# A modulation vector summed on VectorE instead of TensorE, in a two-layer fp32 transformer kernel

## The chip, the cores and the metric

The program runs on one core of one Trainium2 chip. The metric is the device time of one execution in microseconds (us). The kernel before takes 1998.46 us, the median of three runs (1994.62 to 2003.45). The profile below is of one further execution, which took 1997.8 us; its span, from the first to the last recorded instruction, is 1996.1 us.

## The reference, cut to what matters

Two layers act on x of 256 tokens by 2048 features. The first layer begins with an adaptive norm: a vector c of 2048 numbers, through silu and a large matrix, gives a shift, a scale and a gate of 2048 numbers each. All is fp32.

```python
mod = jax.nn.silu(c) @ w_ada + b_ada                 # w_ada: 2048 x 6144
shift, scale, gate = jnp.split(mod, 3, axis=-1)
h = _rms_norm(x, g_norm) * (1.0 + scale[:, None, :]) + shift[:, None, :]
proj = h @ w_in                                      # w_in: 2048 x 9296
```

What follows (two attentions, an output product, a second layer with a recurrent mixer, latent attention and a feed-forward block) is not touched by the change. Only shift and scale matter here, that is 4096 columns of w_ada (33.6 MB); the gate's columns are read and summed later, in the old way.

## The kernel before, in words

**Engines.** Each engine has its own instruction list, and semaphores order them. SyncE (SP) issues all large loads, in the order in which they are written. TensorE (PE) multiplies. ScalarE (ACT) copies each loaded piece of a weight to a rounded high part (`high`, L1474). GpSimd (POOL) subtracts that from the piece to get the low part (`low_part`, L545). VectorE (DVE) splits activations in the same way (L1883, L1884).

**Pieces.** A product in fp32 accuracy is made of three products of high and low parts (L865, L866, L867). A weight piece is 512 rows of 512 columns (1 MB; four slots in `WR`, two in `WH`). ScalarE and GpSimd handle it in two halves of 128x1024.

**The head of the kernel.** The 2048 features are taken in four quarters of 512. For quarter q the kernel needs shift and scale of those 512 features, that is 1024 columns of w_ada over all 2048 rows. It reads them in eight pieces, numbers 8q to 8q+7, each 256 rows by 1024 columns in two loads of 512 KB, into four slots `ada_w` (`ada_quarter`, L605). `mod_piece` (L934) multiplies each piece on TensorE: four matmuls of 512 columns, each with 32 stationary columns that all hold silu(c), so that four groups of PSUM partitions hold four partial rows. After the eighth piece ScalarE copies the bank to `mod_row` (L1533), `mod_cols` (L942) turns the row into columns, VectorE adds the bias (L1875) and forms the gain (L1878), ScalarE scales the four transposed blocks of x (L1537), and VectorE splits them into `HX` (L1883, L1884). Then four weight pieces of `w_in` for those 512 rows can be multiplied (`piece`): (q,0) has 128 columns, (q,1) and (q,2) have 512 and give transposed output, (q,3) has 512 and gives token-major output. Below, "piece (q,i)" is one of these, and "the end of the head" is the last product of piece (3,3). After it follow the remaining columns of `w_in`, with the same three helpers.

**What sets the order.** It is written out by hand. On TensorE the products of the next quarter's modulation stand between the four pieces (3, 2, 2 and 1 of them). On SyncE the loads of the next quarter's eight modulation pieces stand between the loads of this quarter's pieces. A modulation slot is free again when `ada_done` has counted its piece, a `WR` slot when `piece_done` has. GpSimd and ScalarE take the pieces of `w_in` in order; the high part of piece n waits for TensorE to have done piece n-2.

**The start.** Before the first quarter, SyncE also issues 24 small parameter loads (L625 to L633), x is normalised, and TensorE transposes x through a diagonal matrix (L976), which ScalarE copies to `xT` (L1500).

Of the kernel before, what the change touches and what calls it, by code (L numbers as in the profile page):

```python
# [21 lines left out]
ALU = mybir.AluOpType  # L22
ACT = mybir.ActivationFunctionType
# [3 lines left out]
P = 128  # L27
# [3 lines left out]
KT = D // P  # L31
# [15 lines left out]
CH = 512  # L47
# [87 lines left out]
def build(nc, a, out):  # L135
    ctx = ExitStack()
    with ctx:
# [38 lines left out]
        def at(off, *shape):  # L176
            n = int(np.prod(shape))
            assert off + n <= ARENA, (off, n)
            v = arena[:, off:off + n]
            used[0] = off + n  # L180
            if len(shape) == 1:
                return v
            names = "abcd"[:len(shape)]
            return v.rearrange(f"p ({' '.join(names)}) -> p {' '.join(names)}",
                               **{m: s for m, s in zip(names[1:], shape[1:])})
# [45 lines left out]
        mod_row = at(4096, CH)  # L231
        CA = at(4608, KT, 32)
# [6 lines left out]
        half_col = small[:, 400:402]  # L239
        ones = level0T  # L240
# [335 lines left out]
        def _(sp):  # L576
# [57 lines left out]
            ada_quarter(0, 4, 8)  # L634
            for q in range(4):
                in_piece(q, 0)
                in_piece(q, 1)
                if q < 3:
                    ada_quarter(q + 1, 0, 3)
                in_piece(q, 2)  # L640
                if q < 3:
                    ada_quarter(q + 1, 3, 5)
                in_piece(q, 3)
                if q < 3:
                    ada_quarter(q + 1, 5, 8)
# [197 lines left out]
        def _(pe):  # L843
# [82 lines left out]
            def mod_piece(n):  # L926

                i = n % 8
                pe.wait_ge(ada_in[n % 4], 32 * (n // 4 + 1))
                if i == 0 and n >= 8:  # L930
                    pe.wait_ge(mod_ready, n // 8)
                for g in range(4):
                    o = slice(32 * g, 32 * g + 32)
                    last = pe.matmul(BANK[0][o, :], CA[:, 2 * i + g // 2, :], ada_w[n % 4][:, g * CH:(g + 1) * CH],  # L934
                                     start=i == 0, stop=i == 7)
                last.then_inc(ada_done, 1)

            def mod_cols(m):

                pe.wait_ge(row_took, m + 1)  # L940
                for j in range(4):
                    last = pe.matmul(BANK[0][:, 2 * j:2 * j + 2], mod_row[:, j * P:(j + 1) * P], half_col,  # L942
                                     start=True, stop=True)
                last.then_inc(mod_cols_ready, 1)
# [54 lines left out]
            pe.wait_ge(c_wide, 1)  # L999
            for n in range(4):  # L1000
                mod_piece(n)

# [7 lines left out]
            for n in range(4, 8):  # L1010
                mod_piece(n)
            for q in range(4):
                more = 8 * (q + 1)
                mod_cols(q)
                for i, (token, first, width) in enumerate(((False, 1, P), (False, 4, CH), (False, 6, CH), (True, 2, CH))):
                    if q < 3:
                        for n in range(*((0, 3), (3, 5), (5, 7), (7, 8))[i]):
                            mod_piece(more + n)
                    piece(n_in + 4 * q + i, q, token, first, width)
                    if q == 3 and i == 1:  # L1020
                        pe.wait_ge(kiT_taken, 1)
                        for t in range(TT):
                            last = pe.transpose(BANK[0][:, t * P:t * P + P], KIT[:, t * P:(t + 1) * P], ident[:])
                        last.then_inc(ki_ready, 1)
# [47 lines left out]
            pe.wait_ge(c_wide, 2)  # L1072
# [24 lines left out]
            pe.wait_ge(row_took, 5)  # L1097
# [357 lines left out]
        def _(act):  # L1455
# [75 lines left out]
            for q in range(4):  # L1531
                act.wait_ge(ada_done, 8 * (q + 1))
                act.activation(mod_row, BANK[0][:, :], ACT.Copy).then_inc(row_took, 1)  # L1533
                high(n_in + 4 * q)
                act.wait_ge(mod_ready, q + 1)
                for k in range(4 * q, 4 * q + 4):
                    act.activation(xT[:, k, :], xT[:, k, :], ACT.Identity, bias=mod[:, k:k + 1],  # L1537
                                   scale=gs[:, k:k + 1]).then_inc(x_scaled, 1)
                high(n_in + 4 * q + 1)
                if q == 3:  # L1540
                    act.wait_ge(piece_done, n_in + 13)
                    act.activation(KIT, BANK[1][:, 0:L], ACT.Copy).then_inc(kiT_taken, 1)
                high(n_in + 4 * q + 2)
                high(n_in + 4 * q + 3)
# [278 lines left out]
        def _(dve):  # L1823
# [34 lines left out]
            spread_c(CA)  # L1858
            own.link(dve.tensor_tensor(half_col, group_col[:, 0:2], group_col[:, 2:4], ALU.add))
            norm_dve(0)  # L1860
            make_diag(0)
            dve.wait_ge(colsT_ready, 1)
# [9 lines left out]
            for q in range(4):  # L1872
                o = slice(4 * q, 4 * q + 4)
                dve.wait_ge(mod_cols_ready, q + 1)
                own.link(dve.tensor_tensor(two_rows(mod[:, 0:2 * KT])[:, :, o],  # L1875
                                           BANK[0][:, 0:8].rearrange("p (j h) -> p h j", h=2),
# [471 lines left out]
```

## Time and profile before

| what | value |
|---|---|
| median of three runs | 1998.46 us |
| the profiled execution's own time | 1997.8 us |
| its span | 1996.1 us |
| TensorE busy | 1900.8 us (95% of the span) |
| GpSimd busy | 1322.8 us (66%) |
| VectorE busy | 893.0 us (45%) |
| ScalarE busy | 810.7 us (41%) |
| end of the head | 168.7 us after the start |

Busy time is the sum of an engine's recorded instructions. A recorded duration begins when the instruction is taken up by its engine, so it can contain a time in which the engine is held up. The granted clock (PEclk) is the mean clock that TensorE was given in a stretch, 1.00 being 2.4 GHz. In the timeline view, "x8" merges eight neighbouring instructions of one line; an fp32 matmul leaves two records. "idle before" names what the engine waited for.

### The profile page before, as it was taken

What the parts mean: (1) busy time and instruction counts of PE and PEld (TensorE: products, weight loads), DVE (VectorE), ACT (ScalarE), POOL (GpSimd) and SP (SyncE); (2) the same over time, 40 slices, a digit from 0 to 9 for tenths busy, and PEclk for the clock granted to TensorE, in tenths of its full rate; (3) what the DMA queues carried; (4) which work ended last, traced back from release to release, by engine and by line L of the source; (5) the groups of instructions that cost most, each with busy time, mean ns of one, the idle gap of its engine ahead of it and who ended that gap; (6) DMA issues with size and microseconds to landing.
All of it is one profiled execution on the core that took longest, in us unless ns stands there. A gap on an engine that the chain in (4) does not pass through costs nothing.

```text
span 1996.1 us, 32360 instructions
## 1 busy us (share of the span) xinstructions
PE 1900.8 (95%) x13023; PEld 1590.4 (80%) x13023; DVE 893.0 (45%) x1122; ACT 810.7 (41%) x1095; POOL 1322.8 (66%) x677
## 2 busy tenths in 40 slices
PE   5889999999989899999999999999999999999997
PEld 2668878888658798877699877888888888888886
DVE  1005547560442424556644251654455555733323
ACT  3234444444444454333422343443443433434333
POOL 2448878888139499863544386798888888844442
PEclk9899999999999999999999999999999999999999
DMA  9985545555765356543100145555555555555553
GB/s 340 360 294 169 190 159 178 190 190 190 288 209 178 116 169 208 183 136 128 43 25 4 46 168 168 169 186 181 182 187 189 189 182 182 184 195 198 195 190 126
DMA packets 174434, 352.60 MB, mean 177 GB/s; under 512 B 6736, under 2 KB 19422, under 8 KB 171774
## 3 DMA queue, kind: packets, MB, share of 16 engines
q1 hardware_dynamic: 173437, 346.94, 52.4%
q10 hardware_dynamic: 896, 4.20, 0.5%
q8 instruction: 78, 1.28, 0.3%
q14 instruction: 23, 0.18, 0.0%
HBM read 349.02 MB, written 2.10 MB: 176 GB/s over the span
## 4 chain that ended last, share of the span: by engine, by line
PE 59%; POOL 20%; issue 18%; DVE 2%; ACT 1%; POOLq 0%; DVEq 0%; ACTq 0%
PE bank L911 21%; POOL WL L545 19%; PE bank L913 10%; PE bank L865 6%; PE bank L866 6%; PE bank L867 6%; PE bank L1257 5%; PE bank L1177 1%; PE bank L1187 1%; PE bank L1220 1%; PE bank L393 0%; POOLq L544 0%; DVE arena L2192 0%; POOL arena L812 0%; PE bank L1364 0%
## 5 line engine op out<-in xcount | busy, mean ns | idle before, releaser
L545 POOL TENSOR_TENSOR WL<-WR,WH 128x1024 fp32r<-128x1024 f32 (+2 forms) x516 | 1227.8, 2390 | 495.2 <-ACT WH L1474 493.9
L1474 ACT ACTIVATE WH<-WR 128x1024 fp32r<-128x1024 f32 (+2 forms) x560 | 577.3, 1037 | 815.6 <-PE bank L867 451.8
L911 PE MATMUL bank<-HX,WH 128*128 128x512 f32 x1840 | 651.8, 399 | 6.9 <-POOL WL L545 5.3
L913 PE MATMUL bank<-HX,WL 128*128 128x256 f32 x1840 | 516.6, 281 | 0.0
L911 PEld LDWEIGHTS bank<-HX,WH 128*128 128x128 f32 x1840 | 345.8, 188 | 93.8 <-issue 6.0
L865 PE MATMUL bank<-WH,HX 128*128 128x512 f32 (+2 forms) x864 | 340.2, 394 | 11.3 <-POOL WL L545 6.3
L913 PEld LDWEIGHTS bank<-HX,WL 128*128 128x128 f32 x1840 | 347.6, 189 | 0.0
L866 PE MATMUL bank<-WL,HX 128*128 128x512 f32 (+2 forms) x864 | 332.5, 385 | 0.0
L867 PE MATMUL bank<-WH,HX 128*128 128x512 f32 (+2 forms) x864 | 332.5, 385 | 0.0
L865 PEld LDWEIGHTS bank<-WH,HX 128*128 128x128 f32 x864 | 163.7, 189 | 48.1 <-issue 13.3
L866 PEld LDWEIGHTS bank<-WL,HX 128*128 128x128 f32 x864 | 163.9, 190 | 31.3 <-issue 1.9
L867 PEld LDWEIGHTS bank<-WH,HX 128*128 128x128 f32 x864 | 163.7, 190 | 31.2
L2037 DVE TENSOR_REDUCE arena<-bank 128x256 f32<-128x512 f32 x115 | 71.5, 684 | 251.9 <-PE bank L913 251.9
L865 PE MATMUL bank<-WH,AH 128*128 128x512 f32 x352 | 136.9, 389 | 0.0
L866 PE MATMUL bank<-WL,AH 128*128 128x512 f32 x352 | 136.9, 389 | 0.0
L867 PE MATMUL bank<-WH,AL 128*128 128x512 f32 x352 | 136.9, 389 | 0.0
L545 DVE TENSOR_TENSOR WL<-WR,WH 128x1024 fp32r<-128x1024 f32 x44 | 53.9, 1226 | 159.0 <-ACT WH L1474 159.0
L1960 DVE TENSOR_SCALAR arena<-arena,small 128x128 f32<-128x128 f32 x64 | 63.7, 1065 | 47.8 <-ACT small L1482 47.8
L2275 DVE SCALAR_TENSOR_TENSOR arena<-arena,cols 128x256 f32<-128x256 f32 x44 | 83.3, 1950 | 1.5
L865 PEld LDWEIGHTS bank<-WH,AH 128*128 128x128 f32 x352 | 66.1, 188 | 13.8
L867 PEld LDWEIGHTS bank<-WH,AL 128*128 128x128 f32 x352 | 66.1, 188 | 13.7
L866 PEld LDWEIGHTS bank<-WL,AH 128*128 128x128 f32 x352 | 66.1, 188 | 13.5
(292 smaller groups left out, 1954.1 us busy)
## 6 DMA issues: line engine op xcount, KB each, us to landing
WR<-in_w_in SPq DMA_DIRECT2D x96, 1024.0 KB, 5.0
WR<-in_ffn_w_gate SPq DMA_DIRECT2D x44, 1024.0 KB, 5.1
WR<-in_ffn_w_up SPq DMA_DIRECT2D x44, 1024.0 KB, 5.2
WR<-in_ffn_w_down SPq DMA_DIRECT2D x44, 1024.0 KB, 5.1
arena<-in_w_ada SPq DMA_DIRECT2D x64, 512.0 KB, 9.8
WR<-in_w_out SPq DMA_DIRECT2D x32, 1024.0 KB, 5.1
WR<-in_w_ada SPq DMA_DIRECT2D x16, 1024.0 KB, 5.1
WR<-in_w_in SPq DMA_DIRECT2D x12, 768.0 KB, 4.3
```

Source lines behind the costliest of these rows:

```text
L545: eng.tensor_tensor(half(WL, n % NSLOT, *w), half(WR, n % NSLOT, *w), half(WH, nth(n) % 2, *w), ALU.subtract).then_inc(ready, 1)
L865: pe.matmul(out, stat[0], mov[0], start=start, stop=False, skip_group_check=True)
L866: pe.matmul(out, stat[0], mov[1], start=False, stop=False, skip_group_check=True)
L867: return pe.matmul(out, stat[1], mov[0], start=False, stop=stop, skip_group_check=True)
L911: pe.matmul(bank[:, :].rearrange("p (h n) -> p h n", h=2), wh[:, k, o], HX[:, :, kk, :], start=kk == 0, stop=False, skip_group_check=True)
L913: last = pe.matmul(bank[:, 0:L], wl[:, k, o], HX[:, 0, kk, :], start=False, stop=kk == KT - 1, skip_group_check=True)
L1177: last = pe.matmul(BANK[h // 2][:, (h % 2) * L:(h % 2 + 1) * L], w[h // 2][:, k, (h % 2) * stride:(h % 2) * stride + P], CT[:, c0 + k, :], ...
L1257: last = pe.matmul(o[h, q, :], x(h, q), y(h, q), start=(n == 0), stop=(n == len(terms) - 1))
L1474: act.activation(half(WH, nth(n) % 2, *w), half(WR, n % NSLOT, *w), ACT.Copy).then_inc(hi_ready, 1)
L1960: last = dve.tensor_scalar(v, v, hr[:, g:g + 1], None, ALU.mult)
L2037: dve.tensor_reduce(dst, BANK[bank][:, :].rearrange("p (h n) -> p n h", h=2), AX_X, ALU.add).then_inc(ready, 1)
L2275: last = dve.scalar_tensor_tensor(out=CV[:, f, :], in0=RAWF[:, f, 0:L], scalar=w(0), in1=CV[:, f, :], op0=ALU.mult, op1=ALU.add)
```

## The change

Three things change, all in the head.

1. The modulation sums leave TensorE. `mod_add` on VectorE takes each of the 32 pieces in two instructions of 128x1024: the loaded half times silu(c) as a scalar per partition, added to `mod_sum` (the first of a quarter is a plain multiply). After eight pieces `mod_sum` holds 128 partial sums for each of 1024 columns. `mod_cols` multiplies it with a column of ones: eight matmuls of 2 columns in the place of four. `mod_piece`, the copy of the bank to `mod_row` and the widening of silu(c) (`spread_c(CA)`) go.
2. SyncE's order is new: pieces (q,0) and (q,1) are loaded ahead of the last modulation pieces of quarter q, and (q,2), (q,3) among the first ones of quarter q+1.
3. ScalarE makes the high parts of (q,0) and (q,1) before it waits for the gains of quarter q.

```diff
-            ada_quarter(0, 4, 8)
-            for q in range(4):
+            in_piece(0, 0)
+            ada_quarter(0, 4, 7)
+            in_piece(0, 1)
+            ada_quarter(0, 7, 8)
+            for q in range(1, 4):
+                ada_quarter(q, 0, 2)
+                in_piece(q - 1, 2)
+                ada_quarter(q, 2, 4)
+                in_piece(q - 1, 3)
+                ada_quarter(q, 4, 6)
                 in_piece(q, 0)
+                ada_quarter(q, 6, 7)
                 in_piece(q, 1)
-                if q < 3:
-                    ada_quarter(q + 1, 0, 3)
...
+                ada_quarter(q, 7, 8)
+            in_piece(3, 2)
+            in_piece(3, 3)
...
             def mod_cols(m):
 
-                pe.wait_ge(row_took, m + 1)
+                pe.wait_ge(ada_done, 8 * (m + 1))
                 for j in range(4):
-                    last = pe.matmul(BANK[0][:, 2 * j:2 * j + 2], mod_row[:, j * P:(j + 1) * P], half_col,
-                                     start=True, stop=True)
+                    for h in range(2):
+                        o = slice(h * CH + j * P, h * CH + (j + 1) * P)
+                        last = pe.matmul(BANK[0][:, 4 * j + 2 * h:4 * j + 2 * h + 2], mod_sum[:, m % 2, o], ones[:, 0:2],
+                                         start=True, stop=True)
...
             for q in range(4):
-                act.wait_ge(ada_done, 8 * (q + 1))
-                act.activation(mod_row, BANK[0][:, :], ACT.Copy).then_inc(row_took, 1)
                 high(n_in + 4 * q)
+                high(n_in + 4 * q + 1)
                 act.wait_ge(mod_ready, q + 1)
...
+            def mod_add(n):
+
+                q, i = n // 8, n % 8
+                total = mod_sum[:, q % 2, :]
+                dve.wait_ge(ada_in[n % 4], 32 * (n // 4 + 1))
+                for k in range(2):
+                    w = ada_w[n % 4][:, k * 2 * CH:(k + 1) * 2 * CH]
+                    cc = cs[:, 2 * i + k:2 * i + k + 1]
+                    ins = (dve.tensor_scalar(total, w, cc, None, ALU.mult) if i + k == 0 else
+                           dve.scalar_tensor_tensor(out=total, in0=w, scalar=cc, in1=total, op0=ALU.mult, op1=ALU.add))
+                    if k == 0:
+                        own.link(ins)
+                ins.then_inc(ada_done, 1)
+                dve.wait_ge(ada_done, n + 1)
+
+            mod_add(0)
+            mod_add(1)
             norm_dve(0)
             make_diag(0)
+            for n in range(2, 6):
+                mod_add(n)
...
             for q in range(4):
                 o = slice(4 * q, 4 * q + 4)
+                for n in range(8 * q if q else 6, 8 * q + 8):
+                    mod_add(n)
                 dve.wait_ge(mod_cols_ready, q + 1)
```

VectorE's list between the first quarter's split and the second quarter's gain, before. `HX` is the split activation, `small` holds the gains, `cols` the parameters.

```order
L1883 CAST HX<-arena 128x512
L1884 TENSOR_TENSOR HX<-arena,HX 128x512
L1875 TENSOR_TENSOR small<-bank,cols 128x2x4
L1878 SCALAR_TENSOR_TENSOR small<-small,cols 128x4
L1883 CAST HX<-arena 128x512
```

The same place in the changed kernel, where `arena` in the new rows is both `mod_sum` and the loaded slot `ada_w`.

```order
L1883 CAST HX<-arena 128x512
L1884 TENSOR_TENSOR HX<-arena,HX 128x512
L1847 TENSOR_SCALAR arena<-arena,small 128x1024
L1848 SCALAR_TENSOR_TENSOR arena<-arena,small 128x1024 x15
L1875 TENSOR_TENSOR small<-bank,cols 128x2x4
L1878 SCALAR_TENSOR_TENSOR small<-small,cols 128x4
L1883 CAST HX<-arena 128x512
```

Sixteen instructions of 128x1024 now stand between the split of one quarter and the gain of the next.

SyncE's list behind the small parameter loads, before. The loads of 128x2x512 are halves of w_ada's pieces, those of 128x4x128 are pieces (q,0), those of 128x4x512 the other pieces of w_in.

```order
L605 DMA arena<-in_w_ada 128x2x512 x8
L581 DMA WR<-in_w_in 128x4x128
L581 DMA WR<-in_w_in 128x4x512
L605 DMA arena<-in_w_ada 128x2x512 x6
L581 DMA WR<-in_w_in 128x4x512
L605 DMA arena<-in_w_ada 128x2x512 x4
L581 DMA WR<-in_w_in 128x4x512
```

And in the changed kernel.

```order
L579 DMA WR<-in_w_in 128x4x128
L603 DMA arena<-in_w_ada 128x2x512 x6
L579 DMA WR<-in_w_in 128x4x512
L603 DMA arena<-in_w_ada 128x2x512 x6
L579 DMA WR<-in_w_in 128x4x512
L603 DMA arena<-in_w_ada 128x2x512 x4
L579 DMA WR<-in_w_in 128x4x512
L603 DMA arena<-in_w_ada 128x2x512 x4
L579 DMA WR<-in_w_in 128x4x128
```

Piece (0,0) is now loaded ahead of w_ada's pieces 4 to 6, and piece (0,1) ahead of piece 7; pieces (1,0) and (1,1) come ahead of w_ada's last two and last piece of their quarter.

## Rows read from the trace of the kernel before

**Rows 1.** The page's first part: busy time, share of the span, instructions.

```profile
PE 1900.8 (95%) x13023; PEld 1590.4 (80%) x13023; DVE 893.0 (45%) x1122; ACT 810.7 (41%) x1095; POOL 1322.8 (66%) x677
```

**Rows 2.** Windows from each quarter's gain to the next, then the head's end.

```profile
core 0: us, PE busy (x) PEld busy (x) DVE busy (x) ACT busy (x) POOL busy (x), PEclk, DMA share, GB/s
40.00:80.30 40.30, 34.52 (x204) 23.00 (x204) 2.16 (x5) 9.24 (x13) 15.61 (x8) 0.79 1.02 369
80.30:112.60 32.30, 29.19 (x204) 20.98 (x204) 2.47 (x6) 9.23 (x13) 15.63 (x8) 0.95 1.02 367
112.60:143.30 30.70, 27.87 (x204) 20.17 (x204) 2.48 (x6) 9.23 (x13) 15.69 (x8) 1.00 0.80 282
143.30:168.70 25.40, 21.97 (x134) 20.14 (x134) 12.08 (x16) 13.88 (x21) 20.50 (x9) 0.87 0.50 166
```

**Rows 3.** Timeline of VectorE from 36 to 180 us: start, duration, what.

```profile
39.42 0.47 DVE L1878 SCALAR_TENSOR_TENSOR small<-small,cols 128x4 f32<-128x4 f32 x1
...
80.29 0.17 DVE L1875 TENSOR_TENSOR small<-bank,cols 128x8 f32<-128x8 f32 x1 [37.02 <-PE bank L942]
80.49 0.16 DVE L1878 SCALAR_TENSOR_TENSOR small<-small,cols 128x4 f32<-128x4 f32 x1
...
83.34 0.69 DVE L1884 TENSOR_TENSOR HX<-arena,HX 128x512 fp32r<-128x512 f32 x1
...
143.54 0.16 DVE L1878 SCALAR_TENSOR_TENSOR small<-small,cols 128x4 f32<-128x4 f32 x1
```

**Rows 4.** Timeline of TensorE around the last quarter's start and end.

```profile
142.35 0.95 PE L942 MATMUL bank<-small,arena 128*128 128x2 f32 x8
146.06 0.39 PE L865 MATMUL bank<-HX,WH 128*128 128x256 f32 x1 [2.77 <-DVE HX L1884]
...
149.44 0.55 PE L865 MATMUL bank<-HX,WH 128*128 128x256 f32 x1 [0.66 <-POOL WL L545]
...
168.32 0.39 PE L867 MATMUL bank<-WH,HX 128*128 128x512 f32 x1
```

**Rows 5.** Groups by line and shape from 36 to 150 us.

```profile
L545 POOL TENSOR_TENSOR WL<-WR,WH 128x1024 fp32r<-128x1024 f32 x20 | 47.5, 2390 | 40.5 <-ACT WH L1474 40.4
...
L934 PE MATMUL bank<-arena 128*32 128x512 f32 x208 | 30.6, 688 | 12.5 <-DMA arena<-in_w_ada 11.4 <-DVE small L1878 1.1
...
L545 POOL TENSOR_TENSOR WL<-WR,WH 128x256 fp32r<-128x256 f32 x8 | 5.7, 731 | 52.3 <-ACT WH L1474 52.3
```

**Rows 6.** VectorE groups by line and shape, whole run.

```profile
L545 DVE TENSOR_TENSOR WL<-WR,WH 128x1024 fp32r<-128x1024 f32 x44 | 53.9, 1226 | 159.0 <-ACT WH L1474 159.0
...
L2246 DVE CAST AH<-arena 128x1024 fp32r x8 | 5.5, 687 | 0.0
...
L2139 DVE SCALAR_TENSOR_TENSOR Bv<-Bv,RA 128x2048 f32<-128x2048 f32 x1 | 2.3, 2291 | 0.0
```

**Rows 7.** Timelines of VectorE and GpSimd, 1700 to 1715 us, in the feed-forward block.

```profile
1704.45 2.62 DVE L2246 CAST AH<-arena 128x1024 fp32r<-128x1024 f32 x1 [0.21 <-DVE arena L2287]
1707.10 3.32 DVE L2247 TENSOR_TENSOR AL<-arena,AH 128x1024 fp32r<-128x1024 f32 x1
1710.34 2.88 DVE L2246 CAST AH<-arena 128x1024 fp32r<-128x1024 f32 x1
1713.26 3.31 DVE L2247 TENSOR_TENSOR AL<-arena,AH 128x1024 fp32r<-128x1024 f32 x1
...
1703.59 11.88 POOL L545 TENSOR_TENSOR WL<-WR,WH 128x1024 fp32r<-128x1024 f32 x4 [0.43 <-ACT WH L1474]
```

**Rows 8.** A scalar_tensor_tensor of 256 columns with GpSimd busy beside it.

```profile
L2086 DVE SCALAR_TENSOR_TENSOR arena<-arena,cols x24: 472/2370/2718, 781.2 to 895.4; 128x256 f32 x24
```

**Rows 9.** Windows of 10 us.

```profile
20.00:30.00 10.00, 7.97 (x46) 5.85 (x47) 1.09 (x8) 1.79 (x3) 0.00 (x0) 1.00 0.92 310
30.00:40.00 10.00, 8.47 (x73) 5.47 (x71) 0.64 (x2) 4.27 (x9) 1.41 (x2) 1.00 1.05 368
...
70.00:80.00 10.00, 10.00 (x63) 8.05 (x62) 0.00 (x0) 1.21 (x3) 1.43 (x2) 1.00 1.05 389
```

**Rows 10.** Timeline of ScalarE: the last copy of x's transposes.

```profile
33.94 0.60 ACT L1500 ACTIVATE arena<-bank 128x512 f32<-128x512 f32 x1 [0.41 <-PE bank L976]
```

**Rows 11.** TensorE's timeline, piece (0,1), which follows waits: first and later products.

```profile
57.08 0.58 PE L865 MATMUL bank<-HX,WH 128*128 128x256 f32 x1
...
60.87 0.41 PE L867 MATMUL bank<-HX,WL 128*128 128x256 f32 x1
...
61.49 0.28 PE L867 MATMUL bank<-HX,WL 128*128 128x256 f32 x1
```

More of the change, by code:

```diff
@@ L230, in build @@
         kin_g = at(24992, IDX_DIM)
-        mod_row = at(4096, CH)
-        CA = at(4608, KT, 32)
+        mod_sum = at(4096, 2, 2 * CH)
         ada_w = [at(8192 + PK * CH * i, PK * CH) for i in range(4)]
@@ L238, in build @@
         group_col = ident[:].rearrange("p (g m) -> p g m", m=32)[:, :, 0]
-        half_col = small[:, 400:402]
         ones = level0T
@@ L633, in _ @@
             sp.dma_start(kin_g, a["k_norm_idx"][0:1, :].to_broadcast([P, IDX_DIM])).then_inc(params_in, 16)
-            ada_quarter(0, 4, 8)
-            for q in range(4):
+            in_piece(0, 0)
[8 more added lines that the diff above has]
+                ada_quarter(q, 4, 6)
                 in_piece(q, 0)
+                ada_quarter(q, 6, 7)
                 in_piece(q, 1)
-                if q < 3:
-                    ada_quarter(q + 1, 0, 3)
[L640 to L645, printed above, removed]
+                ada_quarter(q, 7, 8)
+            in_piece(3, 2)
+            in_piece(3, 3)
             with sp.Fori(1, 8) as j:
@@ L924, in ada_piece @@
                 last.then_inc(piece_done, 1)
[L926 to L936, printed above, removed]
             def mod_cols(m):
-                pe.wait_ge(row_took, m + 1)
+                pe.wait_ge(ada_done, 8 * (m + 1))
                 for j in range(4):
-                    last = pe.matmul(BANK[0][:, 2 * j:2 * j + 2], mod_row[:, j * P:(j + 1) * P], half_col,
-                                     start=True, stop=True)
+                    for h in range(2):
+                        o = slice(h * CH + j * P, h * CH + (j + 1) * P)
+                        last = pe.matmul(BANK[0][:, 4 * j + 2 * h:4 * j + 2 * h + 2], mod_sum[:, m % 2, o], ones[:, 0:2],
+                                         start=True, stop=True)
                 last.then_inc(mod_cols_ready, 1)
@@ L997, in _ @@
             pe.transpose(BANK[7][:, 0:KT], c_rows[0:KT, :], ident[0:KT, 0:KT]).then_inc(cT_ready, 1)
-            pe.wait_ge(c_wide, 1)
-            for n in range(4):
-                mod_piece(n)
             pe.wait_ge(params_in, PARAM_DMAS * 16)
@@ L1009, in _ @@
                 to_feature(X, g, 4, 0, scaled=True)
-            for n in range(4, 8):
-                mod_piece(n)
             for q in range(4):
-                more = 8 * (q + 1)
                 mod_cols(q)
                 for i, (token, first, width) in enumerate(((False, 1, P), (False, 4, CH), (False, 6, CH), (True, 2, CH))):
-                    if q < 3:
-                        for n in range(*((0, 3), (3, 5), (5, 7), (7, 8))[i]):
-                            mod_piece(more + n)
                     piece(n_in + 4 * q + i, q, token, first, width)
@@ L1070, in _ @@
                         last.then_inc(headT_ready, 1)
-            pe.wait_ge(c_wide, 2)
+            pe.wait_ge(c_wide, 1)
             pe.wait_ge(act_took, ACT_RKV)
@@ L1096, in _ @@
             turn_y(1)
-            pe.wait_ge(row_took, 5)
+            pe.wait_ge(row_took, 1)
             gate_chunk(0)
@@ L1538, in _ @@
                                    scale=gs[:, k:k + 1]).then_inc(x_scaled, 1)
-                high(n_in + 4 * q + 1)
                 if q == 3:
@@ L1857, in _ @@
             dve.wait_ge(cs_ready, 1)
-            spread_c(CA)
-            own.link(dve.tensor_tensor(half_col, group_col[:, 0:2], group_col[:, 2:4], ALU.add))
+            def mod_add(n):
[13 more added lines that the diff above has]
+            mod_add(1)
             norm_dve(0)
             make_diag(0)
+            for n in range(2, 6):
+                mod_add(n)
             dve.wait_ge(colsT_ready, 1)
@@ L1873, in _ @@
                 o = slice(4 * q, 4 * q + 4)
+                for n in range(8 * q if q else 6, 8 * q + 8):
+                    mod_add(n)
                 dve.wait_ge(mod_cols_ready, q + 1)
                 own.link(dve.tensor_tensor(two_rows(mod[:, 0:2 * KT])[:, :, o],
-                                           BANK[0][:, 0:8].rearrange("p (j h) -> p h j", h=2),
+                                           BANK[0][:, 0:16].rearrange("p (j h two) -> p h j two", h=2, two=2)[:, :, :, 0],
                                            two_rows(col("b_ada", 0, 2 * KT))[:, :, o], ALU.add))
```

## The prediction

> **What bounds the kernel now.** I read the page's busy shares first: TensorE is busy 95% of the span [rows 1], so outside the head it sets the time, and the change touches only the head. So the question is when the head ends. I then cut the head at each quarter's gain [rows 2]. Column by column the reader is to see: the transfers run at 369 and 367 GB/s with a share of 1.02 in the first two stretches and 282 in the third; TensorE is busy 34.5 of 40.3, 29.2 of 32.3 and 27.9 of 30.7 us; GpSimd is busy 15.6 us in each; VectorE only 2.2 to 2.5 us. Transfers and TensorE are both near their end, and VectorE is nearly empty. A stretch of 10 us with full transfers shows 389 GB/s [rows 9]; a quarter needs 8.39 MB of w_ada and 3.41 MB of w_in, 11.80 MB, which is 30.3 us at that rate. The gains are made at 39.9, 80.65 and 143.7 us [rows 3], and the last product of the head ends at 168.7 us [rows 4].
>
> **What the change removes.** TensorE loses the modulation's products: 208 records, 30.6 us, between 36 and 150 us [rows 5]. Of this little reaches the end by itself, because the transfers leave only 30.3 us as the least for a quarter against cadences of 32.3 and 30.7. ScalarE's copy of the bank and its wait go, too. All that could be won is set by the transfers, and is worked out under the third rival.
>
> **What it adds.** Per quarter VectorE gets one multiply and 15 multiply-adds of 128x1024. No row has a multiply-add of exactly this shape. The one of 2048 columns takes 2.291 us and an addition-type instruction of 1024 columns takes 1.226 [rows 6], so a multiply-add of 1024 lies between 1.15 (half of 2.291) and 1.226; I take 1.22, and 0.03 for each wait on its own semaphore (80.29 + 0.17 to 80.49 [rows 3]). The multiply takes 0.69, as the cast of the same shape [rows 6]. Sum: 0.69 + 15 x 1.25 = 19.4 us. Behind it stands a chain in which VectorE does nothing else: eight matmuls of 2 columns, twice the four that take 0.95 [rows 4], with the hand-over 2.0 us; the gain, from 80.29 to 80.65, 0.36; ScalarE's scaling and the split, until 84.03, 3.4 us [rows 3]. Together 25.2 us for a quarter if nothing holds VectorE up. That is less than the 30.3 of the transfers, so taken alone the change would be hidden behind them.
>
> **What holds it up.** GpSimd makes the low parts in the same 114 us: 20 of 2.39 us and 8 of 0.73 [rows 5], 15.6 us in each quarter [rows 2]. In the feed-forward block both engines work at once on the same shapes [rows 7]. A VectorE instruction with two inputs in SBUF that takes 1.226 by itself [rows 6] there takes 3.31 and 3.32, the cast 2.62 and 2.88 in place of 0.69; the four GpSimd instructions take 11.88 in place of 4 x 2.39 = 9.56. The excess of 2.3 is a cast and a tensor_tensor and a cast, 0.6 + 1.1 + 0.6. So the engines take turns, instruction by instruction, and each waits for the whole of the other's. The multiply-add does the same: with 256 columns it has a median of 2.37 us beside GpSimd against a least of 0.472 [rows 8]. The price of a GpSimd instruction that meets a multiply-add is therefore its full 2.39 us on VectorE's chain.
>
> The Trainium skill says this as a rule that speaks against the change (SBUF — State Buffer, "Who interferes with whom"): an instruction of VectorE with two SBUF inputs and a GpSimd instruction that reads SBUF exclude each other for their whole length. By that rule the sum is the one below; if only casts and multiplies excluded GpSimd, it would be the third rival's.
>
> The cadence of a quarter is then 25.2 plus what GpSimd does while VectorE has work. All 15.6 us may meet it: 40.8. Or GpSimd fills the 3.5 us in which VectorE waits for the eight matmuls and for ScalarE's first two scalings: 37.3. Pieces (q,0) and (q,1) now get their low parts before the gain, among the last multiply-adds, and the high part of (q,2) waits for TensorE to have done half of (q,0), so its low parts begin when the next quarter's adds do. Little falls into the gap; I take 39.5. VectorE no longer waits for loads, as 39.5 is more than 30.3; the transfers wait for it.
>
> **The first quarter.** At 20.4 us pieces 0 to 3 have arrived as before (there VectorE keeps up: 2.5 us a piece against 2.7 for its transfer). Now (0,0), pieces 4 to 6, (0,1) and piece 7 must come, 5.5 MB; 3.1 MB arrive by 30 us and the rest at 0.37 MB/us by 36.5 [rows 9]. ScalarE is free at 34.5 [rows 10] and makes high parts at once; GpSimd follows from 35.3 with 0.73, 0.73, 2.39, 2.39. The two adds of piece 7 meet them: 36.5 + 2.5 without a collision, two of 2.39 more with both. With the eight matmuls and the gain this is 41.3 to 46.2; I take 44.5, against 39.9 before: +4.6 us.
>
> **The last quarter's products.** Before, 2.4 us passed from the gain to the first product, then 22.6 to the end [rows 4]. The narrow piece ran from 146.06 to 148.8, there was a wait of 0.66 for GpSimd, and (3,1) ran to 157.3 at a lower clock (0.87 over the stretch [rows 2]). Piece (0,1) shows the size: after waits its products come at 0.21 us, and at 0.12 from 61.4 on [rows 11], 4.3 us at 1.2 GHz and then 2.4. In the changed kernel TensorE waits longer before the gain, so this is met once, but (3,1) is ready: 2.7 + 6.9 + 6.0 + 5.6 = 21.2, a gain of 1.4.
>
> **The sum.** The last gain comes at 44.5 + 3 x 39.5 = 163.0 against 143.7. The head ends at 163.0 + 2.4 + 21.2 = 186.6 against 168.7, +17.9 us, and nothing behind it changes. On the profiled execution's 1997.8 us this is 2015.7, predicted as 2016. The median of the runs shown is 0.7 us above that execution, which changes nothing. The own range: with 41.3, 37.3 and 21.2 the head ends at 176.8, with 46.2, 40.8 and 22.6 at 193.6; so 2006 to 2023.
>
> **The rivals.** What a measurement of this kernel can tell from no change is about 0.5%, 10 us.
>
> First, the engines share instead of taking turns: each slows the other, and a meeting costs half. The cadence is 25.2 + 7.8 = 33.0, the head ends at 44.5 + 99 + 23.6 = 167.1, -1.6 us: 1996. For it speaks only that no row has this instruction at 1024 columns beside GpSimd; rows 7 speak against it. 6%.
>
> Second, TensorE's clock. It now works about 21 of 39.5 us per quarter and waits for the rest. Should it stay at 1.2 GHz, its 19.3 us of products (1.7 + 6.0 + 6.0 + 5.6) become 38.6, and with the 2.0 for the columns and the 3.5 until the first product the cadence is 44, bound by TensorE: 44.5 + 132 + 2.4 + 38.6 = 217.5, +49, 2046. Against it: after a wait the clock came back within 4.3 us of work [rows 11]. 5%.
>
> Third, on the other side: the multiply-add does not exclude GpSimd's subtraction, or GpSimd's work falls almost wholly into VectorE's waits. Then the transfers bound each quarter at 30.3, the first gain comes at 41.3, the last at 132.2, and the head ends at 155.8: -12.9, 1985. It is the case if a quarter's meetings cost under 5 us; the change breaks even where they cost 8.3 of the 15.6 (44.5 + 3 x 33.5 + 23.6 = 168.6). Half of GpSimd's work would have to miss VectorE, which is idle 3.5 us in a quarter. 7%. The Trainium skill advises about 358 GB/s for transfers from HBM (SBUF — State Buffer, "Summary: rules for kernel authors"); by it a quarter is 33.0 us and this rival's estimate 1993. The trace has 389, so the rival keeps 1985.
>
> **How the numbers follow.** The forecast has 82%; of it about 76 points lie above 2008.5 and 6 below. Faster by over 0.5% (below 1988.5) is the third rival: 7%. Within 0.5%: the first rival and the forecast's lower edge, 12%. Slower: 76 and the second rival's 5, 81%. The range 2002 to 2024 holds the forecast with a little on either side for how runs scatter, about 8 in 10; the rivals lie outside.
>
> **What would show it.** The multiply-adds of 128x1024 come in two sizes, about 1.22 and 3.3 to 3.6 us, with a mean near 2.2; GpSimd's 2.39 becomes longer, too. The gains lie about 39.5 us apart, VectorE is busy or held nearly all of a quarter's time, and the transfers fall to about 300 GB/s. TensorE has a gap of over 10 us per quarter that ends with VectorE's `ada_done`. Wrong would be: every multiply-add at 1.22 with VectorE waiting for w_ada (third rival), a mean near 1.7 (first), or products at 0.21 us all through a quarter (second). Were the last gain at 163 and the end of the head not 23.6 us later, my tail would be wrong.

## The result, and the profile after

The changed kernel takes 2025.6 us in the median of four runs (2021.2 to 2032.7), against 2001.0 us for the kernel before in four (1994.6 to 2005.4). The ratio is 1.0143, 95% interval 1.0116 to 1.0170: 1.4% slower, 23 to 34 us; the two medians lie 24.7 us apart. Forecast were 2016 us and a range of 2002 to 2024: the direction was right, the size was too small, and the median lies 1.6 us above the range.

The profiled execution took 2032.7 us, its span is 2031.0. First the windows from one gain to the next, then the head's end; the columns are those of [rows 2], which they answer.

```profile
core 0: us, PE busy (x) PEld busy (x) DVE busy (x) ACT busy (x) POOL busy (x), PEclk, DMA share, GB/s
47.80:89.80 42.00, 24.82 (x148) 23.43 (x148) 33.74 (x22) 9.06 (x12) 20.45 (x8) 0.74 0.82 284
89.80:130.50 40.70, 24.36 (x148) 22.97 (x148) 35.16 (x22) 9.06 (x12) 21.38 (x8) 0.75 0.82 287
130.50:171.10 40.60, 24.49 (x148) 23.10 (x148) 33.78 (x22) 9.06 (x12) 20.95 (x8) 0.75 0.67 235
171.10:194.80 23.70, 21.28 (x136) 20.27 (x137) 10.60 (x15) 12.00 (x20) 15.82 (x7) 0.84 0.40 134
```

A quarter lasts 42.0, 40.7 and 40.6 us, where it lasted 40.3, 32.3 and 30.7. VectorE, which was busy 2.2 to 2.5 us, is now busy or held 33.7 to 35.2; the same eight GpSimd instructions, 15.6 us before, take 20.5 to 21.4; the transfers have fallen from 369 to 284 GB/s. The granted clock is 0.74 to 0.75 of full. Next the multiply-adds of the whole run (count, least, median and longest duration in ns, what the engine waited for before them) and GpSimd's low parts from 50 to 150 us.

```profile
L1848 DVE SCALAR_TENSOR_TENSOR arena<-arena,small x60: 1276/1285/3317, 12.7 to 163.8; 128x1024 f32<-128x1024 f32 x60
...
  DMA arena<-in_w_ada: 9.5, 5
```

```profile
L543 POOL TENSOR_TENSOR WL<-WR,WH 128x1024 fp32r<-128x1024 f32 x16 | 48.7, 3072 | 48.8 <-ACT WH L1456 48.8
...
L543 POOL TENSOR_TENSOR WL<-WR,WH 128x256 fp32r<-128x256 f32 x4 | 5.5, 1402 | 2.5 <-ACT WH L1456 2.5
```

A multiply-add takes 1.28 us when it is alone and up to 3.32 beside GpSimd; GpSimd's 2.39 [rows 5] has become 3.07 in the mean. Both are held by the other. One instruction of each, from the middle of a run of such meetings, in the third quarter:

```profile
97.37 3.38 POOL L543 TENSOR_TENSOR WL<-WR,WH 128x1024 fp32r<-128x1024 f32 x1
98.52 3.31 DVE L1848 SCALAR_TENSOR_TENSOR arena<-arena,small 128x1024 f32<-128x1024 f32 x1
```

The next two begin at 100.72 and 101.87, so a pair lasts 3.35 us, where one after the other would need 1.28 + 2.39 = 3.67. The engines take turns, but a meeting costs VectorE 2.03 us (3.31 - 1.28) and not the full 2.39. The timeline of VectorE, with the gains that answer to [rows 3]:

```profile
37.61 6.06 DVE L1848 SCALAR_TENSOR_TENSOR arena<-arena,small 128x1024 f32<-128x1024 f32 x2 [1.87 <-DMA arena<-in_w_ada]
47.41 0.17 DVE L1875 TENSOR_TENSOR small<-bank,cols 128x8 f32<-128x8 f32 x1 [3.73 <-PE bank L934]
47.60 0.16 DVE L1878 SCALAR_TENSOR_TENSOR small<-small,cols 128x4 f32<-128x4 f32 x1
...
80.59 5.08 DVE L1848 SCALAR_TENSOR_TENSOR arena<-arena,small 128x1024 f32<-128x1024 f32 x2 [2.46 <-DMA arena<-in_w_ada]
...
93.85 32.52 DVE L1848 SCALAR_TENSOR_TENSOR arena<-arena,small 128x1024 f32<-128x1024 f32 x15
...
170.99 0.16 DVE L1878 SCALAR_TENSOR_TENSOR small<-small,cols 128x4 f32<-128x4 f32 x1
```

Fifteen multiply-adds, 19.8 us of work with their waits (15 x 1.32), last 32.5. In the quarter of 42.0 us VectorE also waits 2.5 us for w_ada, and in the last one 1.4, which the forecast had excluded. And before each gain VectorE waits 3.73 us for TensorE's column matmuls. TensorE's timeline shows them, and the start and the end of the last quarter's products, as [rows 4] did:

```profile
85.73 3.58 PE L934 MATMUL bank<-level0T,arena 128*128 128x2 f32 x16 [14.35 <-DVE arena L1848]
...
167.11 3.57 PE L934 MATMUL bank<-level0T,arena 128*128 128x2 f32 x16 [13.36 <-DVE arena L1848]
...
194.36 0.40 PE L869 MATMUL bank<-WH,HX 128*128 128x512 f32 x1
```

The eight matmuls take 3.57 us, in the first quarter after 9.3 us of idle time and in the others after 13 to 14. The granted clock over them, and over the four matmuls of the kernel before (the column behind the instruction counts is PEclk):

```profile
85.73:89.31 3.58, 3.57 (x16) 3.49 (x16) 0.00 (x0) 0.00 (x0) 0.00 (x0) 0.50 1.05 386
142.35:143.30 0.95, 0.95 (x9) 0.86 (x7) 0.00 (x0) 0.00 (x0) 0.00 (x0) 1.00 0.00 0
```

It is 0.50, that is 1.2 GHz, in the changed kernel and 1.00 in the kernel before. The head ends at 194.8 us, 26.1 us later than the 168.7 of before. What is left of the profiled executions' difference of 34.9 us, 8.8, lies behind the head, where both kernels run the same instructions; it is taken up below.

### The profile page after: what moved, and what is told of

The parts are those of the page before. It is cut to its first block, busy times and chain, and to the rows that moved or that the text cites. A ratio compares the mean times of both kernels' runs of the same rounds, so it can differ in the third digit from the quotient of the medians.

```text
span 2031.0 us, 31997 instructions
## 1 busy us (share of the span) xinstructions
PE 1883.4 (93%) x12799; PEld 1604.2 (79%) x12799; DVE 1018.7 (50%) x1184; ACT 810.7 (40%) x1091; POOL 1340.1 (66%) x677
## 4 chain that ended last, share of the span: by engine, by line
PE 59%; POOL 20%; issue 18%; DVE 2%; ACT 1%; POOLq 0%; DVEq 0%; ACTq 0%
PE bank L913 20%; POOL WL L543 20%; PE bank L915 10%; PE bank L867 6%; PE bank L868 6%; PE bank L869 6%; PE bank L1239 5%; PE bank L1159 2%; PE bank L1169 1%; PE bank L1202 1%; PE bank L969 0%; PE bank L391 0%; DVE arena L2192 0%; POOLq L542 0%; DVE arena L2322 0%
## 5 line engine op out<-in xcount | busy, mean ns | idle before, releaser
L543 POOL TENSOR_TENSOR WL<-WR,WH 128x1024 fp32r<-128x1024 f32 (+2 forms) x516 | 1245.2, 2424 | 503.1 <-ACT WH L1456 502.0
L1848 DVE SCALAR_TENSOR_TENSOR arena<-arena,small 128x1024 f32<-128x1024 f32 x60 | 116.0, 1934 | 11.8 <-DMA arena<-in_w_ada 9.5
```

Source lines behind the costliest of these rows:

```text
L543: eng.tensor_tensor(half(WL, n % NSLOT, *w), half(WR, n % NSLOT, *w), half(WH, nth(n) % 2, *w), ALU.subtract).then_inc(ready, 1)
L1848: dve.scalar_tensor_tensor(out=total, in0=w, scalar=cc, in1=total, op0=ALU.mult, op1=ALU.add))
```

## The experiments

The theory after the result: the two engines take turns instruction by instruction, as forecast, and the part that the forecast missed is that the column matmuls run at the lower clock. "Head's end" is the last product of piece (3,3) in the run's profile; a ratio is to the kernel before, timed beside it.

**low_small.** GpSimd's work in the head is made short.

```diff
-            eng.tensor_tensor(half(WL, n % NSLOT, *w), half(WR, n % NSLOT, *w), half(WH, nth(n) % 2, *w),
+            eng.tensor_tensor(cut(half(WL, n % NSLOT, *w)), cut(half(WR, n % NSLOT, *w)), cut(half(WH, nth(n) % 2, *w)),
                               ALU.subtract).then_inc(ready, 1)     # cut: v[:, :, 0:32] in the head
-                wh, wl = view(WH, nth(n) % 2, width), view(WL, n % NSLOT, width)
+                wh = wl = view(WH, nth(n) % 2, width)
```

> The changed kernel, but in the head GpSimd subtracts only 32 columns of each weight piece instead of 512 or 128, and TensorE multiplies the high part in the low part's place (the head's low products are left out). Turn-taking theory: the multiply-adds all come at 1.25 us or less, the gains are 25.2 + 1.7 (the column matmuls took 3.6 us, not 2.0) + about 1.5 of short GpSimd instructions = 28.4 us apart if nothing else binds, so the loads bind at 30.3 to 31; head's end near 43.5 + 3 x 31 + 23.6 = 160 us against 194.8 in the changed kernel, the ratio to the kernel before about 0.995. Rival (VectorE's sums are slow by themselves, or the low clock of TensorE is what costs): gains stay 38 us or more apart, ratio above 1.01.

Measured: ratio 0.9935 (0.9918 to 0.9952), head's end 161.4. The multiply-adds of this run, and the timeline around its second gain:

```profile
L1851 DVE SCALAR_TENSOR_TENSOR arena<-arena,small x60: 1276/1285/1348, 12.7 to 132.2; 128x1024 f32<-128x1024 f32 x60
```

```profile
44.41 0.16 DVE L1881 SCALAR_TENSOR_TENSOR small<-small,cols 128x4 f32<-128x4 f32 x1
...
68.85 2.61 DVE L1851 SCALAR_TENSOR_TENSOR arena<-arena,small 128x1024 f32<-128x1024 f32 x2 [2.33 <-DMA arena<-in_w_ada]
75.19 0.17 DVE L1878 TENSOR_TENSOR small<-bank,cols 128x8 f32<-128x8 f32 x1 [3.73 <-PE bank L937]
75.39 0.16 DVE L1881 SCALAR_TENSOR_TENSOR small<-small,cols 128x4 f32<-128x4 f32 x1
```

No multiply-add is above 1.35 us, VectorE waits for w_ada (2.33 us), and the gains are 31.0 us apart. The meetings with GpSimd are worth 33.4 us of head (194.8 - 161.4), more than the whole loss. VectorE's sums alone are fast enough.

**psum.** The same sums with only one tensor input in SBUF.

```diff
-                total = mod_sum[:, q % 2, :]
+                total = BANK[0][:, :]
...
+                for k in range(4):
+                    w = ada_w[n % 4][:, k * CH:(k + 1) * CH]
+                    kk = 4 * (i % 4) + k
+                    dst = mod_sum[:, q % 2, (i // 4) * CH:(i // 4 + 1) * CH] if kk == KT - 1 else total
...
+                           dve.scalar_tensor_tensor(out=dst, in0=w, scalar=cc, in1=total, op0=ALU.mult, op1=ALU.add))
```

> The changed kernel with the running sum in PSUM: w_ada is read as eight pieces of 512 rows by 512 columns, VectorE takes each in four multiply-adds of 512 columns whose second tensor input is PSUM bank 0, and only the last of 16 writes to mod_sum. So only one tensor input lies in SBUF. Turn-taking theory: these adds do not meet GpSimd; each takes 0.69 to 0.72 us, 32 of them 23 us, with 3.7 + 0.4 + 3.4 behind them 30.5 us a quarter, so the loads bind at 31; first gain near 45, head's end 45 + 3 x 31 + 23.6 = 161.6 us, ratio to the kernel before 0.995 to 0.997. Rival (any VectorE instruction with an SBUF tensor input and this much work is held by GpSimd, or the sheer work on VectorE costs): mean of an add above 1.1 us, gains 40 us or more apart, ratio above 1.01.

Measured: ratio 0.9997 (0.9973 to 1.0022), head's end 166.5, 28.3 us before the changed kernel's. Its multiply-adds, and VectorE's and GpSimd's groups from 50 to 150 us:

```profile
L1850 DVE SCALAR_TENSOR_TENSOR bank<-arena,small,bank x112: 747/756/757, 12.2 to 137.0; 128x512 f32<-128x512 f32 x112
```

```profile
L1850 DVE SCALAR_TENSOR_TENSOR bank<-arena,small,bank 128x512 f32<-128x512 f32 x83 | 62.7, 756 | 3.1 <-DMA arena<-in_w_ada 0.2
...
L543 POOL TENSOR_TENSOR WL<-WR,WH 128x1024 fp32r<-128x1024 f32 x19 | 45.0, 2383 | 55.2 <-ACT WH L1456 55.2
```

None of 112 adds is longer than 0.757 us, and GpSimd is back at 2.38: a multiply-add with one SBUF tensor input doesn't meet it. Those 112 also write to PSUM. The last add of each sum writes to SBUF and isn't held either, so it is the input that counts (from 35 to 150 us); nor is it the width, since adds of 256 columns are held in [rows 8]:

```profile
L1850 DVE SCALAR_TENSOR_TENSOR arena<-arena,small,bank 128x512 f32<-128x512 f32 x7 | 5.2, 748 | 0.2
```

The quarters are 32.6 us apart, not 31, since an add takes 0.756 and not 0.69, so that VectorE's chain binds: 32 x 0.79 + 3.7 + 0.4 + 3.4 = 32.8. That miss is 4.9 us of head (166.5 against 161.6), 0.25%; a head 2.2 us shorter than before is a ratio of 0.999, which the interval holds. This answers to the rule of the Trainium skill that the prediction drew on (SBUF — State Buffer, "Who interferes with whom"), by which a VectorE instruction with two SBUF inputs contends with a GpSimd instruction that reads SBUF. The trace agrees: up to 3.32 us with two such inputs, 0.757 at most with one.

**warm.** Idle-time matmuls ahead of the column matmuls.

```diff
+                for k, n in ((5, 12), (6, 12), (7, 9)):
+                    pe.wait_ge(ada_done, 8 * m + k)
+                    warm(n)                       # n matmuls of ident by ident into unread columns
                 pe.wait_ge(ada_done, 8 * (m + 1))
```

> The changed kernel with 33 idle-time matmuls of 128x128 in front of each mod_cols (after the adds of pieces 5, 6 and 7 of the quarter), written to columns of bank 0 that nobody reads. Clock theory: the eight column matmuls of a quarter take 1.9 us in place of 3.57, so each gain comes 1.7 us sooner, the first products of the quarter run at 0.12 us; head's end 4 x 1.7 + 1.5 = 8 us sooner, near 187 us, ratio to the kernel before about 1.009. Rival (matmuls of 2 columns into one bank cost that much at any clock): 3.6 us stays, head's end near 194, ratio 1.013. Turn-taking itself is not touched: multiply-adds beside GpSimd stay at 3.5 us.

Measured: ratio 1.0101 (1.0082 to 1.0120), head's end 191.0, half of what was expected. The first quarter's column matmuls took 1.95 us, the others 3.50, 3.26 and 2.72. TensorE's timeline (products left out) around its second gain:

```profile
78.41 2.27 PE L931 MATMUL bank<-ident 128*128 128x128 f32 x18 [1.62 <-DVE arena L1856]
83.02 3.50 PE L942 MATMUL bank<-level0T,arena 128*128 128x2 f32 x16 [2.34 <-DVE arena L1856]
```

TensorE was idle for 2.34 us between the fillers and the columns. The granted clock over the column matmuls of the four quarters:

```profile
43.78:45.73 1.95, 1.95 (x16) 1.87 (x16) 0.00 (x0) 0.00 (x0) 0.00 (x0) 0.96 1.05 385
83.02:86.52 3.50, 3.50 (x16) 3.41 (x16) 0.00 (x0) 0.00 (x0) 0.00 (x0) 0.52 1.05 386
123.71:126.96 3.25, 3.25 (x16) 3.17 (x16) 0.00 (x0) 0.00 (x0) 0.00 (x0) 0.56 1.05 387
164.09:166.81 2.72, 2.72 (x16) 2.64 (x16) 0.00 (x0) 0.00 (x0) 0.00 (x0) 0.68 0.00 0
```

The time follows the clock, so the clock theory stands. It does not follow the idle time just before: that was 2.02 us in the first quarter, 2.34 in the next two and 4.22 in the last. Fillers that leave a gap do not make the clock sure.

**warm2.** More fillers: `((5, 14), (6, 14), (7, 15))`, and `warm(9)` behind the columns.

> The changed kernel with more idle-time matmuls: 14, 14 and 15 behind the adds of pieces 4, 5 and 6 of a quarter and 9 behind the column matmuls. In the first run with such matmuls a gap of 1.6 to 4.2 us was left ahead of the column matmuls, which took 1.95, 3.50, 3.26 and 2.72 us. Clock theory: with the gap closed they take 1.9 to 2.1 in each quarter and the first products 0.12; gains about 39 us apart, head's end near 186, ratio 1.008. Rival (the matmuls' length does not hang on the clock before them): over 3 us again.

Measured: ratio 1.0101 (1.0063 to 1.0139), head's end 185.8. The column matmuls' records (two for each matmul), and one quarter's:

```profile
L942 PE MATMUL bank<-level0T,arena x64: 251/251/272, 44.0 to 163.0; 128*128 128x2 f32 x64
```

```profile
83.05 1.95 PE L942 MATMUL bank<-level0T,arena 128*128 128x2 f32 x16 [0.37 <-DVE arena L1857]
```

All are at 0.251 us against 0.353 in the changed kernel, 1.95 us for the eight, with a granted clock of 1.00 over them in the second quarter; the gains are 39.1 us apart, and the head ends 9.0 us sooner. With the clock that the forecast took for granted, the head ends near where the forecast had it (186.6), which is in part luck: the first gain is 1.9 us later than forecast, the three quarters together 1.1 and the tail 1.6 us shorter. The ratio is that of warm, whose head ended 5.2 us later, so what the second set of fillers adds is shown by the traces and not by the times.

**sums_only.** VectorE's sums, old orders of SyncE and ScalarE (the first and the fourth hunk of the diff undone).

> VectorE's sums with the load order and ScalarE's order of the kernel before. Turn-taking theory: the same GpSimd work meets the same adds, so the gains stay about 41 us apart; head's end 195 to 197 us (piece (q,1)'s low parts come after the gain), ratio to the kernel before 1.012 to 1.015, within 0.2% of the changed kernel. Rival (the new order of loads, which puts GpSimd's work beside the adds, is what costs): gains 33 to 36 us apart, ratio below 1.006.

Measured: ratio 1.0103 (1.0082 to 1.0125), head's end 186.9. The gains, at 40.9, 81.7, 122.4 and 163.4, are 40.8 us or more apart, so the cadence is not the order's, as the theory said. But the first gain is 6.9 us sooner, which my 195 to 197 had left out, and the ratio lies below the 1.012 to 1.015 expected. The head ends 7.9 us sooner than the changed kernel's, and 3.9 of them are given back at once: behind it TensorE waits 3.7 us for the index keys where the changed kernel went straight on and then waited 1.2, and the next products start at 192.4 against 196.4 us.

This run also shows the multiply that opens a quarter's sum beside GpSimd (GpSimd's low parts begin at 44.05 us, the multiply at 44.21):

```profile
L1843 DVE TENSOR_SCALAR arena<-arena,small x4: 752/2864/2872, 11.9 to 125.7; 128x1024 f32<-128x1024 f32 x4
```

It has one tensor input in SBUF and writes to SBUF, and still takes 2.86 us in place of 0.75, as the casts of [rows 7] did. So two SBUF inputs are what makes the multiply-adds meet GpSimd, but other instructions meet it with one.

**first_old.** The changed kernel with only the first quarter's loads as before (pieces 4 to 7 of w_ada, then (0,0) and (0,1)).

> The changed kernel with one thing undone: in the first quarter w_ada's pieces 4 to 7 are loaded ahead of w_in's pieces (0,0) and (0,1), as before. Theory (putting these two ahead delays piece 7 by their 1.3 MB and brings their low parts beside its adds): first gain 41 to 42.5 us in place of 47.8, later gains still 40.7 to 42 apart, head's end 187.5 to 190 against 194.8, ratio to before 1.009 to 1.011. Rival (the low parts must meet some adds anyway, so the first quarter's saving is given back in the second): first gain early, but the second still near 89.8, head's end 194, ratio 1.013.

Measured: ratio 1.0094 (1.0060 to 1.0127), gains at 41.7, 83.4, 124.1 and 164.8, head's end 188.6. The 6.2 us of the first quarter are kept to the end. So of the changed kernel's loss 6 us come from two loads put ahead of w_ada's in the first quarter.

**order_only.** The kernel before with the new orders, TensorE's sums kept (the first and the fourth hunk alone).

> TensorE's sums of the kernel before with the new load order and ScalarE's new order. Turn-taking theory: without VectorE's adds nothing is lost; piece (q,1) is ready at the gain, which saves 0.7 to 3 us in the last quarter, head's end 164 to 169 us, ratio 0.997 to 1.000. Rival (the order costs): w_ada's pieces come later than TensorE's list wants them, gains 34 us or more apart, head's end above 175, ratio above 1.003.

Measured: ratio 1.0060 (1.0043 to 1.0077), head's end 182.0. I expected no loss, and there are 13 us; the rival was right. SyncE's timeline:

```profile
45.10 6.35 SPq L605 DMA_DIRECT2D arena<-in_w_ada  x4
55.64 0.37 SPq L581 DMA_DIRECT2D WR<-in_w_in  x1
56.05 1.02 SPq L605 DMA_DIRECT2D arena<-in_w_ada  x2
67.46 0.37 SPq L581 DMA_DIRECT2D WR<-in_w_in  x1
```

The load of (1,0), at 55.64, needs the slot of (0,0), and that of (1,1), at 67.46, the slot of (0,1). Pieces of w_ada stand behind each of them in SyncE's list; but TensorE has the products of three of w_ada's pieces ahead of (0,0) and two ahead of (0,1). From 57.1 to 67.5 us nothing is issued. The gains are 41.1, 38.6 and 36.3 us apart. In low_small, with the same order of loads, TensorE has only the four pieces in its list, frees the slots early, and the loads bind at 31.0. So the order is good with VectorE's sums and bad with TensorE's.

**psum_old** and **psum_warm.** The sum in PSUM with the old orders; and with the new orders and fillers (6 and 9 ahead of the columns, 9 behind).

> The sum in PSUM, with the load order and ScalarE's order of the kernel before. The run with VectorE's SBUF sums and the old order had its first gain at 40.9 us against 47.8. If the new order only delays the first quarter: first gain near 42, gains 31 us apart, head's end 42 + 93 + 24 = 159 us, ratio 0.994 to 0.996. Rival (the new order is needed to keep the loads full, since pieces (q,2), (q,3) then wait for free slots less): gains 33 us or more apart, head's end 165 or later, ratio 0.999 or above.

> The sum in PSUM with 15 idle-time matmuls of 128x128 ahead of the column matmuls and 9 behind them, in columns of bank 1 that nobody reads. Clock theory: the eight column matmuls fall from 3.57 to 1.9 us and the quarter's first products run at 0.12 us; the loads bind the quarters at 31 all the same, so only the last quarter gains: 1.7 + 1.5 = 3 us sooner than the same kernel without them, ratio to before 0.993 to 0.996. Rival (the clock is not raised by so little work): the column matmuls stay above 3 us and nothing is gained.

Measured: psum_old 0.9985 (0.9961 to 1.0010), head's end 162.6; psum_warm 0.9954 (0.9930 to 0.9978), head's end 158.2. The gains of psum_old are 31.3, 32.7 and 32.2 us apart, bound by VectorE as in psum; its first is 2.1 us sooner. Head's end and ratio lie between what was expected (159, 0.994 to 0.996) and the rival. In psum_warm the fillers bring the quarters to 31.7, 31.0 and 31.0 and save 8.3 us of head, more than the 3 that I expected, because in psum the quarters were bound by VectorE's chain and not by the loads. TensorE in the last quarter:

```profile
134.18 1.95 PE L942 MATMUL bank<-level0T,arena 128*128 128x2 f32 x16 [0.88 <-DVE arena L1859]
135.99 2.25 PE L931 MATMUL bank<-ident 128*128 128x128 f32 x18
138.96 0.39 PE L867 MATMUL bank<-HX,WH 128*128 128x256 f32 x1 [0.72 <-DVE HX L1895]
139.19 0.28 PE L868 MATMUL bank<-HX,WH 128*128 128x256 f32 x1
139.31 0.28 PE L869 MATMUL bank<-HX,WL 128*128 128x256 f32 x1
```

The columns take 1.95 us and the first products come 0.12 us apart. This is the version that beats both kernels: 0.2 to 0.7% faster than before.

**psum_old_warm.** Both together.

> The sum in PSUM, the old order of loads and of ScalarE's high parts, and idle-time matmuls (15 ahead of the column matmuls, 9 behind). The sum in PSUM with the new order and such matmuls ended its head at 158.2 us, with gains at 42.8, 74.5, 105.6 and 136.6; with the old order and none, at 162.6. If the two savings add: column matmuls 1.95 us, gains 31.0 apart bound by VectorE's 32 adds of 0.79, first gain near 41, head's end 155 to 158 us, ratio to the kernel before 0.993 to 0.996. Rival (with the old order piece (q,1) is late whenever TensorE is faster, as in the 0.46 us gap there): head's end 160 or later, ratio 0.997 or above.

Measured: ratio 0.9977 (0.9952 to 1.0002), head's end 158.2, as without the old order. The first gain is a microsecond sooner (41.9), but piece (0,1) and its successors come late: TensorE waits 1.34 us behind each narrow piece. And behind the head it waits 4.0 us, not 1.4, for the index keys. VectorE's timeline there:

```profile
148.10 2.00 DVE L1895 TENSOR_TENSOR arena<-arena 128x64 f32<-128x64 f32 x1 [9.73 <-ACT arena L1532]
150.14 0.22 DVE L1896 TENSOR_REDUCE small<-arena 128x1 f32<-128x64 f32 x1
...
155.26 6.75 DVE L1902 SCALAR_TENSOR_TENSOR arena<-arena,small 128x64 f32<-128x64 f32 x4 [0.27 <-ACT small L1469]
```

GpSimd is busy without a break from 142.9 to 161.9 us. The small instructions with two SBUF inputs take 1.7 to 2.1 us each, so they stand behind one 2.4 us GpSimd instruction after another; a reduction between them takes 0.22. The savings do not add.

**Behind the head.** Span less head's end is 1827.4 us before and 1836.2 in the changed kernel's profile. In the ten other runs it is 1819.5 (psum_old), 1819.6 (psum_warm), 1821.2, 1825.6, 1826.3, 1830.2, 1830.3, 1831.3, 1832.2 and 1833.4, without a visible relation to the change made. In the changed kernel's profile the surplus lies in the recurrent scan, where PEclk in four windows of 100 us is 0.95, 0.90, 0.98 and 0.93 against 0.98, 0.98, 0.95 and 0.98. The ten spread over 13.9 us and the changed kernel's is 2.8 above the highest of them, so nothing shows that the 8.8 us belong to the change. The head's 26.1 do, and they lie in the measured interval of 23 to 34. What moves the clock in that stage from run to run was not tried.

## Why the prediction was wrong in size

Right was the mechanism and its place. VectorE's sums fit under the transfers by themselves (low_small); they meet GpSimd's low parts instruction by instruction (3.32 us against 1.28), and do so because both tensor inputs of the add lie in SBUF (psum). The tail, from the last gain to the head's end, was forecast at 23.6 and measured at 23.6. The rivals fell: half-price meetings by the adds' 3.3 us (a meeting cost 2.0 of 2.39, not 1.2), the lasting low clock by the products, which recover within each quarter, and the undisturbed sums by all of this.

The step that failed is "eight matmuls of 2 columns, twice the four that take 0.95, with the hand-over 2.0 us". They took 3.57, with the hand-over 3.73. The 0.95 was read from a row in which TensorE came straight from its products [rows 4]. In the changed kernel it comes from a wait of 9 to 14 us, and the granted clock over the eight is 0.50 against 1.00. I had written that TensorE now waits longer before the gain, and charged that to the products behind the gain only. The difference is 1.7 us in each of four quarters, 6.9 us in all; the head's end was missed by 8.2 (194.8 against 186.6). warm2 shows it: with the clock kept up, the eight take 1.95 and the head ends at 185.8. That the other terms come to only 1.3 us is luck, as the list shows: 8 to 9 us charged too low stand against 7.7 charged too high.

The other terms:

- The first gain came at 47.8, not 44.5: 1.7 for the columns, and piece 7's two adds ended at 43.7, not at about 42, since the piece arrived at 37.6 and not at 36.5 and both adds met GpSimd. The prediction named 36.5 + 2.5 and the meetings, and took a value between. first_old shows that the two loads put ahead cost 6.2 us; the prediction had +4.6 for the quarter as a whole.
- A multiply-add alone takes 1.285 us, not 1.22. The prediction said that no row has this shape. That was wrong: the final norm has four multiply-adds of 128x1024 at 1.278 (L2322) in the trace before. Over a quarter it is 1.0 us, and the opening multiply took 0.75 and not 0.69.
- VectorE was to wait for no load. It waited 2.5 us for w_ada in the second quarter and 1.4 in the fourth, 3.8 in all. Why those pieces came late was not followed.
- Against that the meetings cost less than the 14.3 us charged to a quarter. The third took 40.7, and its chain without meetings takes 28.1 (0.75 + 15 x 1.32 + 3.7 + 0.4 + 3.4), so they cost 12.6. The same sum, with the waits for w_ada taken off, gives about 11.4 for the second and 11.2 for the fourth: 7.7 us less than charged over the three. The price was too high: a meeting cost 2.03 us, not "its full 2.39". [Rows 7] had shown this, with 3.31 against 1.226, that is 2.1.
- Two of the three quarters kept within the bound of 40.8, on which the range's upper end was built; the second, with 42.0, did not. Its own range for the head's end was 176.8 to 193.6; the measured 194.8 is 1.2 us above it.
- The 2016 was added up on the 1997.8 us of one execution; the kernel before had a median of 2001.0 beside the changed one. Of the 9.6 us between 2016 and 2025.6, 3.2 come from there. By the medians the change cost 24.7 us where 17.9 were forecast.

So the range was too narrow for a plain reason: the columns' 2.0 had no bounds of its own. The rows at half the clock were in the prediction, for the products [rows 11]; applied to the columns they give 3.8. The trace before even has matmuls of 128x2 at both lengths, 0.251 us a record in the median and 0.352 at most (L1364).

## What to carry to other kernels

- Before work is moved to an idle engine, list what runs beside it and which inputs it reads. Here one operand moved from SBUF to PSUM took away what the old order of loads did not: the adds stayed at 0.756 us beside GpSimd.
- When work is taken from TensorE, price what it keeps at the lower clock too, above all short matmuls on the path; they follow the wait that the change makes.
- A load order is good only with the list of the engine that frees the slots. The same order bound at 31 us a quarter with one list (low_small) and at 36 to 41 with the other (order_only).

## What the runs showed of the hardware that I had not expected

- The time of a matmul of 128 rows by 2 columns in fp32, two records, follows the granted clock: every 0.24 us at 0.96 to 1.00 (1.95 for eight) and every 0.45 at 0.50 (3.57), 1.8 times as long. How long TensorE was idle just before does not tell which it will be: 3.57 came after 4.4 us as after 14.4 (low_small, changed kernel), and in warm 2.34 us went with 3.50 and 4.22 us with 2.72.
- Taking turns is not quite exclusive: with 1.28 and 2.39 us alone, a pair of instructions of the two engines lasts 3.35 and not 3.67.
- A multiply-add of 128x512 with PSUM as second input takes 0.748 to 0.756 us (psum), against 0.692 for the four of the trace before that have PSUM as the first one (L2208); what makes the difference was not tried. Two of them (1.51) are dearer than one of 1024 columns in SBUF (1.285) as long as GpSimd is quiet, and far cheaper when it is not.
